# Four weight-block sums per block pair of the MLP: made in GpSimd's program instead of VectorE's

## The reference, cut to what matters

```python
u = jnp.square(jax.nn.relu(rms_norm(h, norm_pre_mlp) @ w_up))
h = h + rms_norm(u @ w_down, norm_post_mlp)
```

## Time and profile before

| | |
|---|---|
| median of 3 runs | 1738.59 us |
| profiled execution | 1739.95 us, its span 1737.9 us |
| TensorE busy | 1669.0 us, 96% |
| VectorE busy | 1101.5 us, 63% |
| ScalarE busy | 699.5 us, 40% |
| GpSimd busy | 70.4 us, 4% |
| mean granted TensorE clock | 0.98 of full speed |

### The profile page before, as it was taken

How to read it: one execution, slowest core, us unless ns; L and a number is a source line. 1 busy time by engine, 2 the same in 40 slices (tenths; PEclk the granted TensorE clock), 3 DMA queues, 4 the chain that set the end, 5 groups by cost and what they waited for, 6 DMA issues and landing times.

```text
span 1737.9 us, 36308 instructions
## 1 busy us (share of the span) xinstructions
PE 1669.0 (96%) x15770; PEld 1545.0 (89%) x15770; DVE 1101.5 (63%) x1795; ACT 699.5 (40%) x1040; POOL 70.4 (4%) x96
## 2 busy tenths in 40 slices
PE   9999998899899999999999999988998999999988
PEld 8888875599899999998998888756998999999988
DVE  5624875436777777766746257664368777777674
ACT  5432435445433333333543233355354333333332
POOL 0012100000000000000000131000000000000000
PEclk9999999999999999999999998999999999999999
DMA  9412459832926635542372133696339356555421
GB/s 340 148 61 64 172 195 350 312 127 109 358 97 242 242 139 206 200 150 75 126 280 73 62 116 108 238 368 251 127 146 347 109 205 241 196 190 172 152 63 65
DMA packets 61661, 314.01 MB, mean 181 GB/s; under 512 B 7232, under 2 KB 8896, under 8 KB 59328
## 3 DMA queue, kind: packets, MB, share of 16 engines
q1 hardware_dynamic: 53792, 206.51, 33.1%
q0 software_dynamic: 7424, 100.47, 15.9%
q10 hardware_dynamic: 288, 4.72, 0.8%
HBM read 296.34 MB, written 115.80 MB: 237 GB/s over the span
## 4 chain that ended last, share of the span: by engine, by line
PE 83%; DVE 7%; ACT 4%; DMA 3%; issue 2%; POOL 1%; SPq 0%; DVEq 0%; ACTq 0%
PE pair L2104 7%; PE pair L2106 7%; PE pair L2105 7%; PE pair L2092 6%; PE pair L2093 6%; PE pair L2094 6%; PE pair L937 2%; PE pair L939 2%; PE pair L941 2%; PE pair L854 2%; PE pair L1226 2%; PE pair L855 2%; PE pair L856 2%; PE pair L2066 2%; PE pair L919 2%
## 5 line engine op out<-in xcount | busy, mean ns | idle before, releaser
L2104 PE MATMUL pair<-u_hi_part,w_hi_part 128*128 128x288 f32 x1024 | 302.9, 296 | 5.6 <-DVE tmp L2492 4.1
L2106 PE MATMUL pair<-u_hi_part,w_lo_part 128*128 128x288 f32 x1024 | 302.2, 295 | 0.0
L2105 PE MATMUL pair<-u_lo_part,w_hi_part 128*128 128x288 f32 x1024 | 301.8, 295 | 0.0
L2419 DVE TENSOR_TENSOR w_lo_part<-raw,w_hi_part 128x1024 fp32r<-128x1024 f32 (+1 forms) x154 | 174.5, 1133 | 95.8 <-ACT w_hi_part L2208 92.7
L2104 PEld LDWEIGHTS pair<-u_hi_part,w_hi_part 128*128 128x128 f32 x1024 | 192.2, 188 | 7.3 <-DVE tmp L2492 4.6
L2105 PEld LDWEIGHTS pair<-u_lo_part,w_hi_part 128*128 128x128 f32 x1024 | 192.2, 188 | 0.1
L2106 PEld LDWEIGHTS pair<-u_hi_part,w_lo_part 128*128 128x128 f32 x1024 | 192.3, 188 | 0.0
L2208 ACT ACTIVATE w_hi_part<-raw 128x1024 fp32r<-128x1024 f32 (+1 forms) x154 | 148.4, 980 | 79.0 <-PE pair L2094 76.1
L2094 PE MATMUL pair<-x_hi_part,w_lo_part 128*128 128x288 f32 x416 | 122.7, 295 | 0.0
L2092 PE MATMUL pair<-x_hi_part,w_hi_part 128*128 128x288 f32 x416 | 122.6, 295 | 0.0
L2093 PE MATMUL pair<-x_lo_part,w_hi_part 128*128 128x288 f32 x416 | 122.5, 295 | 0.0
(11 more groups left out here) (332 smaller groups left out, 4340.3 us busy)
## 6 DMA issues: line engine op xcount, KB each, us to landing
raw<-w_units SPq DMA_DIRECT2D x210, 512.0 KB, 3.6
ck_out<-ck POOLq DMA_DIRECT2D x16, 3060.0 KB, 15.3
arena<-cv SPq DMA_DIRECT2D x24, 640.0 KB, 8.5
arena<-ck SPq DMA_DIRECT2D x18, 640.0 KB, 9.4
more<-ck SPq DMA_DIRECT2D x18, 640.0 KB, 11.7
tail<-cv SPq DMA_DIRECT2D x18, 640.0 KB, 7.9
h<-ck SPq DMA_DIRECT2D x12, 640.0 KB, 10.1
y_out<-x ACTq DMA_DIRECT2D x2, 2304.0 KB, 9.2
```

The lines of the kernel that those rows point to most:

```text
L2104: nc.tensor.matmul(out, wh[:, cols], UH[:, u, t], start=first and k == 0, stop=False)
L2105: nc.tensor.matmul(out, wh[:, cols], UL[:, u, t], start=False, stop=False)
L2106: mm = nc.tensor.matmul(out, wl[:, cols], UH[:, u, t], start=False, stop=last and k == KD - 1)
L2419: return tt_(dst, src, hi.bitcast(F32), ALU.subtract).then_inc(*up(done, 1))
```

## The change

The two functions leave VectorE's program and stand in GpSimd's, with the same arithmetic and the same buffers. GpSimd's loop over copies becomes a loop over the units and pairs: outer sums of pair s, then the pair's cache copy if it has one, then the inner sums of pair s+1. Waits are added for what VectorE's own order gave before: for both loads of the pair, for the remainders and leading parts of the previous inner sums (before `inner_sum` is written again), for the second sum before the third reads it, and for the split of the pair's first block. What VectorE and ScalarE wait for stays as it was.

```diff
             @block.gpsimd
             def _(pool):
-                for b in range(2, DEC_BATCH):
-                    g = 5 * (b - 2)
-                    pool.wait_ge(*at(*((lin_mm, Q[f"up{g}"] + 1) if g < PLAIN else (prod_mm, NP * (g // 2 - FAST) + 1))))
-                    copy_cache(pool, b)
+                tt_ = nc.gpsimd.tensor_tensor
+
+                def inner_sums(s):
+
+                    i, r = SPLIT.index(("inner", s)), R_OF["up", 2 * s]
+                    a11, a21, a22 = raw(r)[:, 0:KD * P], raw(r + 1)[:, 0:KD * P], raw(r + 1)[:, KD * P:2 * KD * P]
+                    pool.wait_ge(*at(*used_part(w_former(i))))
+                    for q in (r, r + 1):
+                        pool.wait_ge(*at(w_landed[slot_of(q)], 16 * loads(q)))
+                    tt_(w_sum(i, 0), a21, a22, ALU.add).then_inc(*up(s_made, 1))
+                    pool.wait_ge(*at(s_made, 4 * (s - FAST) + 1))
+                    if s > FAST:
+                        pool.wait_ge(*at(w_split, SPLIT.index(("inner", s - 1)) + 1))
+                        pool.wait_ge(*at(w_hi, SPLIT.index(("inner", s - 1)) + 1))
+                    tt_(e_sb[:, :], w_sum(i, 0), a11, ALU.subtract).then_inc(*up(s_made, 1))
+
+                def outer_sums(s):
+
+                    i, r = SPLIT.index(("outer", s)), R_OF["up", 2 * s]
+                    a11, a12, a21 = raw(r)[:, 0:KD * P], raw(r)[:, KD * P:2 * KD * P], raw(r + 1)[:, 0:KD * P]
+                    pool.wait_ge(*at(*used_part(w_former(i))))
+                    pool.wait_ge(*at(s_made, 4 * (s - FAST) + 2))
+                    pool.wait_ge(*at(w_split, SPLIT.index(r) + 1))
+                    tt_(w_sum(i, 0), a12, e_sb[:, :], ALU.subtract).then_inc(*up(s_made, 1))
+                    tt_(w_sum(i, 1), a21, a11, ALU.subtract).then_inc(*up(s_made, 1))
+
+                copies = {5 * (b - 2): b for b in range(2, DEC_BATCH)}
+                for g in range(PLAIN):
+                    if g in copies:
+                        pool.wait_ge(*at(lin_mm, Q[f"up{g}"] + 1))
+                        copy_cache(pool, copies[g])
+                inner_sums(FAST)
+                for s in range(FAST, SLOTS):
+                    outer_sums(s)
+                    for g in (2 * s, 2 * s + 1):
+                        if g in copies:
+                            pool.wait_ge(*at(prod_mm, NP * (s - FAST) + 1))
+                            copy_cache(pool, copies[g])
+                    if s + 1 < SLOTS:
+                        inner_sums(s + 1)
...
                 beside_down(FAST - 1, 1)
-                inner_sums(FAST)
                 t_low("T4", "T4")
...
                 for s in range(FAST, SLOTS):
                     p, i = s - FAST, SPLIT.index(R_OF["up", 2 * s])
-                    outer_sums(s)
                     beside_down(s - 1, 3)
                     split_w(i + 2)
...
                     beside_down(s, 0)
                     beside_down(s, 1)
-                    if s + 1 < SLOTS:
-                        inner_sums(s + 1)
                     split_w(i + 7)
```

More of the change, by code:

```diff
@@ L2521, in beside_down @@
                     add_down(pair[j], *BESIDE[s][j])
[L2523 to L2539, removed]
                 def added(p, m, dst, a, b_, after):
```

## The result

The changed kernel is slower: 1750.14 us against 1741.1 (medians of 20 runs each), ratio 1.0044 with a 95% interval of [1.0031, 1.0057], some 7.7 us. (The medians differ by 9.0; I go by the ratio.) I had forecast no change, within 1735 to 1748. The profiled execution took 1749.88 us, its span 1748.0, 10.1 more than before.

The account below looks back on a forecast made before the run. The prediction took TensorE's block products to bound the kernel, with VectorE's sums beside them. Its terms, 0 + 0 + 0 + 0 on the profiled 1739.95 us, gave a forecast median of 1738.6 us, range 1735 to 1748.

Parts of the forecast that it names:

- What bounds the kernel: In the steady block pairs TensorE is busy 24.00 of 24.00 us and its block products never wait for sums.
- Price of a sum on GpSimd: One 128x512 sum on GpSimd was estimated at 1.26 us, scaled from 128x576 operations.
- The uneven L807: A GpSimd operation of 2.27 us, read as having waited for a VectorE operation on two SBUF inputs.
- Outer sums, inner sums in the steady pairs: Both kinds of sum, 26 times each, were to cost 0 because slack stays positive.
- the slack of 1.25: Time left before product S4 once the outer sums run on GpSimd: 1.25 us, 2.52 before the change.
- Queues moved past: Later block loads, the first now level with the cache copy's request, were to cost 0, with some margin left.
- First pair of a layer: Twice: GpSimd's outer sums end near 474.0, VectorE's near 475.15, so the tightest place gets looser; nothing to gain.
- over 4 us of slack: Inner sums' remainder ends near 541.9, product S1 in the next pair starts at 546.1, so a delay costs 0.
- rival A: GpSimd's outer sums, slow or excluded by VectorE, exceed 1.9 us each; TensorE waits for S4: 19 us, 1758; chance 0.07.
- The sign: The forecast would be wrong if VectorE's instructions got longer than their 0.69 and 1.23 us.

Follow-up runs that it names:

- doubled sums: Changed kernel with each pair's two outer sums made twice on GpSimd; 1786.51 us, ratio 1.0251 to the kernel before.
- e1: Changed kernel with the four sums of each layer's first block pair back on VectorE; 1743.76 us, ratio 1.0007 to the kernel before.
- e2: Only the first block pair of each layer has its sums on GpSimd, the others on VectorE; 1747.93 us, ratio 1.0022 to the kernel before.
- e8c: First pair's sums on VectorE, other pairs' on GpSimd, plus three 128x1024 GpSimd copies where its first inner sums would start; 1748.58 us, one execution.
- e7c: First pair's sums on VectorE, other pairs' on GpSimd, plus three 128x1024 GpSimd zero fills where its first inner sums would start; 1745.76 us, one execution.
- the second: The changed kernel measured again, unaltered, against the kernel before, 12 runs; 1747.02 us, ratio 1.0019.
- sums after T4: Changed kernel, but the first pair's inner sums on GpSimd wait until VectorE's T4 products are made; 1745.09 us, ratio 1.0007 to the kernel before.
- e5: Changed kernel with the first pair's inner sums on VectorE, its outer sums still on GpSimd; 1746.61 us, ratio 1.0019 to the kernel before.
- e6: Changed kernel with the first pair's outer sums on VectorE, its inner sums still on GpSimd; 1746.74 us, ratio 1.0015 to the kernel before.

## Why the prediction was wrong

- **What bounds the kernel:** right. TensorE's block products bound the steady stretch, 260.00 of 260.00 us in both kernels.
- **Price of a sum on GpSimd:** right, 1.29 for 1.26. The uneven L807 was read rightly too: GpSimd's operation waits for VectorE's on two SBUF inputs.
- **Outer sums, inner sums in the steady pairs:** right, cost 0, the leading part at 2.57 for 2.6, and the slack of 1.25 was 1.1 by the doubled sums. (With 1.03 a sum it would be 1.7 by the same working, not the 2.0 that I wrote; nothing hangs on it.)
- **Queues moved past:** right, first load 3.3 us.
- **First pair of a layer: this step failed.** I priced the outer sums alone ("GpSimd starts at 471.4 and ends near 474.0 ... so the tightest place gets looser") with undisturbed durations on both sides, and never listed what VectorE does while GpSimd's four sums run there. In this pair VectorE has no gap: T4 products, `t_low`, `x_lo_part`, two remainders, each on two SBUF inputs. I had taken VectorE's lateness as a sign that the place could only get looser; it was the sign that no slack was left. The inner sums of this pair got no line of their own: their "over 4 us of slack" holds for a pair behind a pair. Here it is 0.35 us at S1, behind the copy into `y` that the forecast didn't list, and the loss is 4.0 us a layer where the collision is full, for the forecast's 0.
- **The exclusion was weighed in one direction.** I asked whether VectorE slows GpSimd's sums (rival A), and only in the steady outer place. The loss came the other way: GpSimd's sums make VectorE's operations 2.07 + 2.15 = 4.2 us longer in one row of work. The Trainium skill (SBUF — State Buffer, section SBUF: two separate sides) names it as mutual; the trace agrees, with 3.87 for 1.80 on VectorE and 2.44 for 1.29 on GpSimd.
- **The clock:** no term of the sum. Behind a wait that cost 2.5 us, 1.5 us more went in the low stretch.
- The sign was named ("if VectorE's instructions got longer than their 0.69 and 1.23 us"), and it is what the rows show, in a place where I had not looked.

The cause is shown by undoing (e1), by doing alone (e2) and by a read that has nothing to do with the sums (e8c against e7c). The size is less sure: two layers at 4.0 us fit the first comparison (7.7) and lie above the second (3.3), though both layers collided in the second's trace. Whether a layer collides hangs on less than 2 us of alignment between TensorE's release and T4; in layer 0 of the changed kernel a low clock just before shifted it by 1.5.

## What to carry to other kernels

Before work moves to GpSimd, list beside each moved operation what VectorE does in that stretch, the loop's first round apart: if it reads two SBUF operands, the two engines' times add up there. A steady state with no idle time says nothing of the loop's first round. And look at the granted clock behind a short new wait of TensorE before pricing it at its length; here a wait of 2.5 us cost 4.0.

## What the runs showed of the hardware

- A run of short VectorE operations is not safe: four of 0.51 us took 3.87 beside GpSimd's two sums, VectorE paying 2.07 us and GpSimd 0.39 (1.57 + 1.39 - 2.57), together nearly the 2.57 of the sums.
- The low clock (0.50 for some 3.4 us) came behind all six waits of 2.4 us at S1, and not behind those of 1.3 to 1.8 us (doubled sums, sums after T4, outer half, copies). The wait's length alone doesn't decide: it came behind a wait of 2.0 us too (layer 0 of the changed kernel, 465.93) and stayed away behind 2.3 to 2.4 us ahead of a plain unit in three runs (at 444.70 in the second trace of the changed kernel, 445.50 in e5, 443.32 in e6). What decides is not shown.
- A GpSimd operation that only writes (three fills, 2.98 us) left VectorE's T4 products at 1.80 in the one execution taken.
- `SCALAR_TENSOR_TENSOR` with two SBUF tensors counts like a `TENSOR_TENSOR`; VectorE's `y` additions with one PSUM operand don't appear stretched beside the sums (0.75 for the one at 525.06, beside the sum at 525.11, and 0.75 without a sum beside it).
- The wait that the profile puts down to the remainders ended 0.1 us behind the copy into `y` that follows them: among neighbours on one engine the releaser named can be the one before the true one.
